# Turning normalised tiles by fp32 products with a diagonal of reciprocal roots, in one decoder layer on one core

## The reference, cut to what matters

```
def rms_norm(x, g):
    y = x * rsqrt(mean(x * x, axis=-1) + EPS)
    return y * g

h = rms_norm(x, norm_mix_pre)
rq, rk, rv, rg, aq, ak, av, gr, ga = split(h @ w_in)
... retention (branch A) and dilated attention (branch B), merged, @ w_out ...
x = x + rms_norm(mix, norm_mix_post)
h = rms_norm(x, norm_ffn_pre)
u = h @ w_ffn_up
f = (gelu(conv(u)[:, :D_FF]) * conv(u)[:, D_FF:]) @ w_ffn_down
x = x + rms_norm(f, norm_ffn_post)
```

## Time and profile before

| | us |
|---|---|
| median of 3 runs (lowest to highest) | 1008.76 (1008.15 to 1011.3) |
| profiled execution | 1009.0 |
| its span, first to last instruction | 1007.2 |
| PE busy | 985.4 (98%) |
| DVE busy | 551.8 (55%) |
| ACT busy | 378.6 (38%) |

### The profile page before, as it was taken

The page is one execution under the profiler, slowest core; times in us unless marked ns, Lnnn a source line. Parts: engine busy times, 40 slices in busy tenths (PEclk is TensorE's granted clock), DMA queues, the critical chain, the costliest instruction groups (busy, mean ns, idle before and its releaser), DMA issues.

```text
span 1007.2 us, 20394 instructions
## 1 busy us (share of the span) xinstructions
PE 985.4 (98%) x7774; PEld 876.2 (87%) x7774; DVE 551.8 (55%) x912; ACT 378.6 (38%) x832; POOL 180.1 (18%) x365
## 2 busy tenths in 40 slices
PE   5999999999999999999999999999999999999997
PEld 4788788779999899999887789999999999777775
DVE  5354125535367877783145677666666666422225
ACT  6333232441543333333133644444444444212413
POOL 2102004034162343445100001000000000000100
PEclk9999999999999999999999999999999999999999
DMA  6734545546796676769635324555545553221323
GB/s 243 267 137 160 175 160 169 190 154 216 254 295 222 217 226 195 225 202 330 207 102 173 109 77 168 178 178 174 176 166 176 172 189 128 85 84 64 121 84 118
DMA packets 40466, 175.36 MB, mean 174 GB/s; under 512 B 6937, under 2 KB 7385, under 8 KB 38865
## 3 DMA queue, kind: packets, MB, share of 16 engines
q1 hardware_dynamic: 25616, 125.78, 36.2%
q0 software_dynamic: 14784, 48.65, 15.1%
HBM read 164.40 MB, written 54.05 MB: 217 GB/s over the span
## 4 chain that ended last, share of the span: by engine, by line
PE 91%; DVE 4%; DMA 2%; ACT 1%; issue 1%; SPq 0%; DVEq 0%; POOL 0%; ACTq 0%
PE bank L1339 11%; PE bank L1340 10%; PE bank L1341 10%; PE bank L1857 9%; PE bank L1858 9%; PE bank L1859 9%; PE bank L1421 6%; PE bank L1427 6%; PE bank L1426 6%; PE bank L1358 3%; PE bank L1321 2%; DMA wraw<-in_weights 1%; PE bank L1756 1%; PE bank L1762 1%; PE bank L1761 1%
## 5 line engine op out<-in xcount | busy, mean ns | idle before, releaser
L1942 DVE TENSOR_TENSOR wlo<-wraw,whi 128x1024 fp32r<-128x1024 f32 x88 | 107.6, 1222 | 277.5 <-ACT whi L839 277.1
L839 ACT ACTIVATE whi<-wraw 128x1024 fp32r<-128x1024 f32 x90 | 95.3, 1059 | 318.1 <-PE bank L1341 208.4
L1857 PE MATMUL bank<-T1h,whi 128*128 128x288 f32 (+1 forms) x704 | 202.4, 288 | 1.8 <-DVE T1l L1952 1.6
L1858 PE MATMUL bank<-T1l,whi 128*128 128x288 f32 (+1 forms) x704 | 203.6, 289 | 0.0
L1859 PE MATMUL bank<-T1h,wlo 128*128 128x288 f32 (+1 forms) x704 | 203.2, 289 | 0.0
L1857 PEld LDWEIGHTS bank<-T1h,whi 128*128 128x128 f32 x704 | 133.0, 189 | 2.2 <-issue 1.8
L1858 PEld LDWEIGHTS bank<-T1l,whi 128*128 128x128 f32 x704 | 132.7, 189 | 0.0
L1859 PEld LDWEIGHTS bank<-T1h,wlo 128*128 128x128 f32 x704 | 132.3, 188 | 0.0
L1339 PE MATMUL bank<-whi,T1h 128*128 128x512 f32 (+1 forms) x288 | 113.8, 395 | 0.5 <-DVE T1l L1952 0.3
L1421 PE MATMUL bank<-T1h,whi 128*128 128x272 f32 x384 | 113.4, 295 | 0.0
L1427 PE MATMUL bank<-T1h,wlo 128*128 128x272 f32 x384 | 111.0, 289 | 0.0
(11 more groups left out here) (302 smaller groups left out, 1818.1 us busy)
## 6 DMA issues: line engine op xcount, KB each, us to landing
wraw<-in_weights SPq DMA_DIRECT2D x142, 512.0 KB, 3.7
out_s_kv_g<-in_cache_kv_g SPq DMA_DIRECT2D x64, 511.0 KB
qbc<-sample_queries POOLq DMA_DIRECT2D x48, 256.0 KB, 4.9
kvk<-in_cache_kv_g POOLq DMA_DIRECT2D x32, 256.0 KB, 4.3
kvv<-in_cache_kv_g POOLq DMA_DIRECT2D x16, 512.0 KB, 8.2
out_s_kv_g<-in_cache_kv_g SPq DMA_DIRECT2D x16, 508.0 KB
S<-in_state_ret POOLq DMA_DIRECT2D x16, 256.0 KB, 3.3
out_s_ret<-S POOLq DMA_DIRECT2D x16, 256.0 KB, 6.0
```

What stands on the lines that cost most here:

```text
L839: nc.scalar.activation(w_halves(s)[0], wraw[:, s % 2, :], ACT.Copy).then_inc(w_hi, 1)
L1857: mm(dst, Wh, T1h[:, k, c], start=k == 0, stop=False)
L1858: mm(dst, Wh, T1l[:, k, c], start=False, stop=False)
L1942: v.tensor_tensor(lo, wraw[:, s % 2, :], hi.bitcast(F), ALU.subtract).then_inc(w_lo, 1)
```

## The change

The turning and the scaling by the reciprocal root become one product. DVE writes a 128x128 diagonal matrix, the identity times the reciprocal roots, and PE multiplies: tile as stationary operand, diagonal as moving operand, both fp32, in place of the transpose.

- Up-projection input, all five tiles: `hidden_gain` multiplies by `gffn` ahead of the root, `hidden_scale` makes only the diagonal. DVE's hand-written order is changed with it. PE turns both halves on one wait. The last tile is turned inside the second half-product (before its k=5), and the waits for it are spread over the next.
- Layer input, tiles 0 and 1: products straight from `xin`. The norm weight is not in them: it is applied to the bank, as a per-partition factor of a column table (`gcol`, 4 KB, a new DMA), by ACT in four pieces of 128 columns for each half and by DVE in four pieces of scalar-times-minus. Tiles 2 to 4 are scaled and transposed as before.
- SP's order at the start is tile 0, identity, weight slot 0, `gcol`, tile 1, `gpre`, tiles 2 to 4. ACT splits slot 0 before tile 1's parts (after tile 0's square), slot 1 after tile 3's square and tile 2's parts.
- Block 0 waits for the first half of each tile only, and for the second halves after its first slot.

```diff
@@ SP
         load_x(0)
+        sp.dma_start(ca_t[:, 0:128], a["tables"][:, 0:128]).then_inc(ident_in, 16)
+        sp.dma_start(wraw[:, 0, :], w_dram[0]).then_inc(w_raw[0], 16)
+        sp.dma_start(gcol[:], a["norm_mix_pre_columns"]).then_inc(gcol_in, 16)
+        load_x(1)
         sp.dma_start(gpre[:], a["norm_mix_pre"].broadcast_to([128, D])).then_inc(gpre_in, 16)
-        sp.dma_start(ca_t[:, 0:128], a["tables"][:, 0:128]).then_inc(ident_in, 16)
-        load_x(1)
-        sp.dma_start(wraw[:, 0, :], w_dram[0]).then_inc(w_raw[0], 16)
@@ ACT, split_evac and the input loop
+            if key[0] == "x" and i < 2:
+                act.wait_ge(gcol_in, 16)
+                for k in range(4):
+                    ins = nc.scalar.activation(Th[:, k0 + k, c], src[:, k, :], ACT.Copy, scale=gcol[:, k0 + k:k0 + k + 1])
+                ins.then_inc(split_hi, 1)
+                return
-            if i == 1:
+            if i == 0:
                 w_split(0)
-            if i == 2:
+            if i == 3:
                 w_split(1)
@@ PE
+                else:
+                    last = mm(b[0:m, k * n:(k + 1) * n], src, by, start=True, stop=True)
         def turn_input(i):
             pe.wait_ge(x_norm, i + 1)
-            turn_wide("x", xn, i, i % 2)
+            if i < 2:
+                for half in range(2):
+                    turn(("x", i, half), [xin[:, i, 128 * k:128 * k + 128] for k in range(4 * half, 4 * half + 4)], 128,
+                         by=x_diag[:, i, :])
+            else:
+                turn_wide("x", xn, i, i % 2)
@@
-            for half in range(2):
-                emptied(pe, ("x", i, half))
+            emptied(pe, ("x", i, 0))
+                if bi == 0 and s == 1:
+                    for i in range(TILES):
+                        emptied(pe, ("x", i, 1))
@@ turn_hidden
+            pe.wait_ge(h_ready, p + 1)
             for half in range(2):
-                pe.wait_ge(h_ready, 2 * p + half + 1)
+                turn(("h2", i, half), [hn[0:r, p % 2, 128 * k:128 * k + 128] for k in range(4 * half, 4 * half + 4)],
+                     r, by=h_diag[0:r, p % 2, 0:r])
+        def last_turned(k):
+            if k == KT - 3:
+                turn_hidden(TILES - 1)
+        def last_head(k):
+            if k % 4 == 0:
+                emptied(pe, ("h2", NORM_ORDER[TILES - 1], k // 4))
-        up_half(1, 0)
-        turn_hidden(TILES - 1)
+        up_half(1, 0, last_turned)
-        head_ready_for(TILES - 1)
-        up_half(0, 1).then_inc(w_used, 1)
+        up_half(0, 1, last_head).then_inc(w_used, 1)
@@ DVE, layer input
+            if i < 2:
+                dve.wait_ge(x_rt, i + 1)
+                step(v.reciprocal(rs_x[:, i:i + 1], rt_x[:, i:i + 1]))
+                v.tensor_scalar(x_diag[:, i, :], ident, rs_x[:, i:i + 1], None, ALU.mult).then_inc(x_norm, 1)
@@ DVE, up-projection input
+        def hidden_gain(p):
+            ...
+            for half in range(2):
+                c = slice(512 * half, 512 * half + 512)
+                v.tensor_tensor(hn[0:r, p % 2, c], xo[0:r, i, c], gffn[0:r, c], ALU.mult)
@@ hidden_scale
-            for half in range(2):
-                c = slice(512 * half, 512 * half + 512)
-                v.scalar_tensor_tensor(hn[0:r, p % 2, c], xo[0:r, i, c], rs, gffn[0:r, c], ALU.mult, ALU.mult).then_inc(h_ready, 1)
+            v.tensor_scalar(h_diag[0:r, p % 2, 0:r], ident[0:r, 0:r], rs, None, ALU.mult).then_inc(h_ready, 1)
@@ DVE's order
         mixed(0)
+        hidden_gain(0)
         second_gain(1)
+        hidden_scale(0)
         mixed(1)
-        hidden_scale(0)
+        hidden_gain(1)
         second_gain(2)
         hidden_scale(1)
+        hidden_lo(0)
         mixed(2)
-        hidden_lo(0)
+        hidden_gain(2)
         first_gain(2)
-        first_gain(3)
         hidden_lo(1)
         hidden_scale(2)
+        first_gain(3)
         second_gain(3)
         mixed(3)
+        hidden_gain(3)
         hidden_lo(2)
+        hidden_scale(3)
         w_split(S_UP + 1)
-        hidden_scale(3)
         second_gain(4)
         mixed(4)
+        hidden_gain(4)
+        hidden_scale(4)
         hidden_lo(3)
-        hidden_scale(4)
         hidden_lo(4)
```

More of the change, by code:

```diff
@@ L305, in build_layer @@
     junk = sb("junk", ATT + 8192, [128, D])
+    x_diag = sb("x_diag", ATT + 9216, [128, 2, 128])
+    gcol = sb("gcol", ATT + 9472, [128, KT])
+    assert ATT + 9472 + KT <= SCR
     rjunk = sb("rjunk", 8960, [128, DV])
@@ L375, in build_layer @@
     njunk = sb("njunk", SCR + 5296, [128, D])
+    h_diag = sb("h_diag", SCR + 6320, [128, 2, 128])
+    assert SCR + 6320 + 256 <= SCR + 6912
     out_split = [sb(f"out_split{n}", 2 * SLOT * n, [128, 2, SLOT], R) for n in range(4)]
@@ L428, in build_layer @@
     ca_in, cr_in, gpre_in, convp_in = sem("ca_in"), sem("cr_in"), sem("gpre_in"), sem("convp_in")
+    gcol_in = sem("gcol_in")
     g2_in, gfin_in, cvs_in = sem("g2_in"), sem("gfin_in"), sem("cvs_in")
@@ L1315, in open_bank, with turn @@
             return P[bank], bank_full[bank]
-        def turn(key, srcs, n, m=128):
+        def turn(key, srcs, n, m=128, by=None):
             b, full = open_bank(key)
             for k, src in enumerate(srcs):
-                last = nc.tensor.transpose(b[0:m, k * n:(k + 1) * n], src, ident[0:n, 0:n])
+                if by is None:
+                    last = nc.tensor.transpose(b[0:m, k * n:(k + 1) * n], src, ident[0:n, 0:n])
+                else:
+                    last = mm(b[0:m, k * n:(k + 1) * n], src, by, start=True, stop=True)
             last.then_inc(full, 1)
@@ L1821, in turn_hidden @@
             i = NORM_ORDER[p]
+            r = rows(i)
+            pe.wait_ge(h_ready, p + 1)
             for half in range(2):
-                pe.wait_ge(h_ready, 2 * p + half + 1)
-                turn(("h2", i, half), [hn[0:rows(i), p % 2, 128 * k:128 * k + 128] for k in range(4 * half, 4 * half + 4)],
-                     rows(i))
+                turn(("h2", i, half), [hn[0:r, p % 2, 128 * k:128 * k + 128] for k in range(4 * half, 4 * half + 4)],
+                     r, by=h_diag[0:r, p % 2, 0:r])
         def out_rows(p, turned):
@@ L1847, in _, with up_half @@
         out_rows(4, {2: 2})
-        def up_half(j, half):
+        def up_half(j, half, amid=None):
             at_, width = UP_HALVES[half]
@@ L1854, in up_half @@
             for k in range(KT):
+                if amid:
+                    amid(k)
                 cut = slice(128 * k, 128 * k + 128)
@@ L1951, in split_evac @@
             hi = Th[:, k0:k0 + 4, c].bitcast(F)
+            if key[0] == "x" and i < 2:
+                for k in range(4):
+                    ins = v.scalar_tensor_tensor(Tl[:, k0 + k, c], src[:, k, :], gcol[:, k0 + k:k0 + k + 1], hi[:, k, :],
+                                                 ALU.mult, ALU.subtract)
+                ins.then_inc(bank_free[USES[key][0]], 1)
+                return
             v.tensor_tensor(Tl[:, k0:k0 + 4, c], src, hi, ALU.subtract).then_inc(bank_free[USES[key][0]], 1)
@@ L1993, in rope @@
                     v.tensor_tensor(x, tc, tn, ALU.add).then_inc(rope_done, 1)
-        dve.wait_ge(gpre_in, 16)
+        dve.wait_ge(ident_in, 16)
         for i in range(TILES + 1):
-            if i < TILES:
+            if i < 2:
+                dve.wait_ge(x_rt, i + 1)
+                step(v.reciprocal(rs_x[:, i:i + 1], rt_x[:, i:i + 1]))
+                v.tensor_scalar(x_diag[:, i, :], ident, rs_x[:, i:i + 1], None, ALU.mult).then_inc(x_norm, 1)
+                if i == 0:
+                    dve.wait_ge(gcol_in, 16)
+            elif i < TILES:
                 r = rows(i)
+                if i == 2:
+                    dve.wait_ge(gpre_in, 16)
                 dve.wait_ge(x_rt, i + 1)
-                if i >= 2:
+                if i >= 4:
                     filled(dve, ("x", i - 2, 1))
@@ L2341, in mixed @@
                 v.scalar_tensor_tensor(xo[0:r, i, c], xo[0:r, i, c], rs, xr[0:r, i, c], ALU.mult, ALU.add).then_inc(x2_ready, 1)
+        def hidden_gain(p):
+            i = NORM_ORDER[p]
+            r = rows(i)
+            if p >= 2:
+                filled(dve, ("h2", NORM_ORDER[p - 2], 1))
+            dve.wait_ge(x2_ready, 2 * p + 2)
+            for half in range(2):
+                c = slice(512 * half, 512 * half + 512)
+                v.tensor_tensor(hn[0:r, p % 2, c], xo[0:r, i, c], gffn[0:r, c], ALU.mult)
         def hidden_scale(p):
@@ L2349, in hidden_scale @@
             step(v.reciprocal(rs, rt_n[0:r, 5 + i:6 + i]))
-            if p >= 2:
-                filled(dve, ("h2", NORM_ORDER[p - 2], 1))
-            for half in range(2):
-                c = slice(512 * half, 512 * half + 512)
-                v.scalar_tensor_tensor(hn[0:r, p % 2, c], xo[0:r, i, c], rs, gffn[0:r, c], ALU.mult, ALU.mult).then_inc(h_ready, 1)
+            v.tensor_scalar(h_diag[0:r, p % 2, 0:r], ident[0:r, 0:r], rs, None, ALU.mult).then_inc(h_ready, 1)
         def hidden_lo(p):
@@ L2519 @@
```

(1 more changed line is left out.)

## The result

| | before | after |
|---|---|---|
| median of 15 runs, us | 1008.94 | 1013.44 |
| lowest to highest | 1008.04 to 1011.3 | 1011.79 to 1014.49 |
| profiled execution, us | 1009.0 | 1014.0 |

The changed kernel is slower: ratio 1.0035, 95% interval 1.0028 to 1.0043. I had forecast 1009.6 in a range to 1011.8, no change. The time lies outside the range.

A forecast was written before the change was run, and what follows sets the result against it. The prediction took PE, with 91% of the chain of waits, as the bound. The start's -0.5 and the second stretch's +1.35 gave +0.85 us, 1009.6 against a median of 1008.76, range 1007.2 to 1011.8.

The forecast's parts named there:

- Gain 0.15 to 0.85; I take 0.5: Start: the last tile of the first slot starts at 21.6 to 22.3 instead of 22.44, 0.5 us gained.
- so 0.66 instead of 0.5: Start, ACT: evacuating a half of tile 1 in four 128-column instructions takes 0.66 us instead of 0.5.
- ACT pieces slow: Rival, start: evacuation pieces at 0.27 us delay squares of tiles 2 to 4 by 1.2; 1010.9 us, chance 0.16.
- 20.75 to 21.4: Start: PE turns tile 4, the sample rows, at 20.75 to 21.4 us, after DVE's scale, against 21.44 before.
- early clock: Rival, start: steady products from 6.45 us raise the clock before 10 us; 1008.2 us, chance 0.17.
- +0.45: Up-projection input, sample tile: products take 0.9 to 1.2 us against about 0.6 for transposes, 0.45 us more.
- the forecast 1.35: Second stretch, around the up-projection's input: added product time less the waits that go, a net loss of 1.35 us.
- nothing at the head: Up-projection's head: tile 1's low halves are ready at 590.95, PE comes at 591.4, so no wait, by 0.4 us.
- three signs that I had named for being wrong: Products not 0.22 us; PE's first slot ending over 1.5 us earlier; a wait over 1 us at the head.
- my own rival: Products cost four transposes or loads do not overlap: 5.5 us in second stretch, about 1 at start; 1016, chance 0.05.
- some 6: Second stretch: if a product costs four transposes, as the skill's rule says, this stretch alone is some 6 us worse.
- the three likely cases: Whole kernel: main forecast 1009.6 us (chance 0.58), early clock 1008.2 (0.17), ACT pieces slow 1010.9 (0.16).

The follow-up runs named there:

- e4: The changed kernel with five dropped 512-column matmuls in PE's wait ahead of turning the layer input's sample tile; 1010.85 us.
- e2: Only the layer-input part of the change, the up-projection as in the kernel before; 1011.28 us, ratio 1.0011 to before.
- e1: Only the up-projection part of the change, the layer input as in the kernel before; 1011.59 us, ratio 1.0018 to before.
- e6: e4 with layer-input tiles 0 and 1 evacuated in one instruction for each half, the norm weight left out for them; 1010.86 us.
- e3: The changed kernel, but the sample tile of the up-projection input scaled and transposed as before; 1013.57 us against the changed kernel's 1013.44.
- e9: The kernel before with five dropped 512-column matmuls in PE's wait near 349 us; 1008.2 us, ratio 0.9983 to before.
- e7: Kernel before; block 0's first slot waits for first halves only, up-projection's last tile by product inside the second half-product, its waits spread; 1008.8 us, ratio 0.9986.
- e10: e7 with five dropped matmuls near 349 us and three ahead of turning the layer input's tile 3; 1007.3 us, ratio 0.9978 to before.
- e11: The changed kernel with dropped matmuls ahead of the sample tile's turning and near 349 us; 1012.39 us, ratio 1.0021 to before.
- e5: e1 with tiles turned by transposes, the reciprocal root left out, diagonals still made and waited for; 1009.54 us, ratio 0.9996 to before.
- e8: e7 with three dropped fp32 products of the identity from 6.90 us on, to warm the clock; 1008.83 us.

## Why the prediction was wrong, step by step

- **"Gain 0.15 to 0.85; I take 0.5"** for the start. Against before's profiled execution it was a loss of 0.5 (e4) to 1.0 (e2), against e1's, with the same old start, of 0.0 to 0.5, the fall of the clock left aside. The failed step is the evacuation "so 0.66 instead of 0.5": I took the 0.17 pitch of the earlier trace rows, two copies without a factor, and kept the 1.09 for four as the upper bound. The pieces take 0.27 each on ACT, so 1.08 a half, and on DVE, where I had given them no price at all, 1.08 instead of 0.64. e6 puts 0.87 us on them, which is the gain that did not come. The rival *ACT pieces slow* had this price ("0.27 apiece") and the later squares (1.03 against its 1.2), at a chance of 0.16. That its 1010.9 is also e4's median is luck: the slack at the head that it gave up was not lost, and the sample tile below was.
- **The clock** stood in no sum, and it costs as much as the pieces and more: 1.51 us in the start (e4 against after). That it does so in the 9 of 15 executions at 0.995 or 0.996 is my reading of the table; only the profiled one and e3's show it. I treated half clock as something of the first microseconds and priced only its rise. The forecast had the sample tile's turning wait for DVE ("20.75 to 21.4"), but gave such a wait no price beyond its length. The rival *early clock* had the rise "before 10 us", close to the measured 10.3, and the sign of the result wrong. The spread of before (1008.15 to 1011.3) was in front of me as noise; it goes with the granted clock of the executions.
- **The sample tile, "+0.45"**: I took its eight transposes at 0.6 us and doubled that for twice the instructions. They take 0.81 until the next matmul (e3), and the 16 instructions of the products take 1.90, 0.12 each, as much as with 128 moving columns: +1.1. With the 0.51 wait that did go, the tile costs 0.63 more than before (1.90 against 1.27) where I had -0.1. This 0.7 is the difference between the forecast 1.35 and the measured 2.15 (e1), and e1's time line has it at that tile. Two other terms were off and cancel: tiles 1 and 2 cost 0.91 each (1.70 against 0.79) instead of 1.05, and the last tile came out 0.3 dearer. That the loads of 128 stationary columns set the price is argued, not shown; the run meant to take the product away (e3) ran into DVE instead.
- **Right in the second stretch**: product 0.11 per instruction, two for each; tile 0 a tie; no wait inside the sample tile; a wait of 0.3 and one of 0.6 (0.4); nothing at the head. None of the three signs that I had named for being wrong appeared: they covered neither a fall of the clock nor the sample tile.
- **The Trainium skill's "4× faster for FP32"** (TensorE: Matmul & The Clock Gate, Terms): here a full tile of products takes 1.70 us, of transposes 0.79, 2.2 times and not 4. For the sample tile it is 2.3 times, 1.90 against 0.81. The measurement decides. By the terms of my own rival the stretch would have been 5.5 + 1.4 us worse, near 7, and not the "some 6" that I wrote.
- **The middle, 0.8 us**, was in no step. In the kernels with the new start the distance from the retention's turning to the attention values is 70.1 to 70.5 us, with the old start 69.7 to 70.05, so the ranges touch and before's profiled execution is the lowest of all. 0.3 of it is one wait of PE for ACT's copy of the retention outputs (0.56 instead of 0.29), and the DMA of the sample queries takes 5.60 us instead of 5.09 on the chain. What ties it to the start was not tried.

The range ended 1.6 us short of the median. It held the three likely cases and the scatter of before, but no bound for a second clock stretch, although one of the three runs before stood 2.5 us over the next.

## What to carry to other kernels

A wait of TensorE among small matmuls can cost more than its length: look at the granted clock behind it before pricing it. Filling it with matmuls whose result is dropped gained about 1.5 us or more in e4, e9 and, over e7's part, e10; in e11 a second filling gained nothing over e4, so measure each. Splitting an evacuation by a per-partition factor cost 0.27 us for each 128x128 piece on both engines: a tile's eight pieces added 1.1 us on ACT and 0.9 on DVE, where the scaling that left DVE had taken 1.28. Move a scale into a product only for the tile whose chain the end waits for, as e7 does, and look up what stands behind it on DVE.

## What the runs showed of the hardware

With a wait filled by 512-column matmuls, 8 of 12 executions (e4), 10 of 11 (e9) and 10 of 11 (e10) had a granted clock of 0.999 or 1.000; but only 3 of 11 in e6, with e4's filling.
- The length of the wait alone does not decide. Near 350 us the clock fell behind waits of 1.05 (before), 1.09, 1.26, 1.42, 1.54 and 1.55 us (after) and held behind 1.15 (e2, e5), 1.24 (e8) and 1.26 (e4). Ahead of the sample tile it fell behind 1.19 (after, e3) and held behind 1.18 (e2). At 600 us it fell behind 1.57 in e9 and held behind the same 1.57 in before and e2.
- A fp32 product with 32 moving and 128 stationary columns takes 0.24 us (1.90 for eight), one with 128 moving columns 0.21 to 0.22.
- A scale of a tile on DVE took 1.93 to 1.98 us instead of 1.27 in every profiled start read for it (before, after, e1, e2, e4, e6, e7, e10, e11): each time the one that begins while POOL is in the second half of slot 1's low half.
- Five dropped matmuls in a wait of 1.2 us moved nothing behind them: the sample tile was turned at 21.98 with them and at 21.93 without.
